# Attention scores as three fp32r products of split operands, in a two-layer gMLP and attention trunk

## The reference

```python
z = h @ w_in[l]                                  # columns: u | v | q | k | value
q = apply_rope(q, cos, sin) * (DIFF_QK_DIM ** -0.5)
k = apply_rope(k, cos, sin)
# 4 heads, each with two halves j of 64 channels; 4 blocks i of 128 query rows
s = jnp.einsum('bqhjd,bkhjd->jbhqk', qb, k)
s = jnp.where(mask, s, NEG_INF)                  # causal by chunks of 64
p = jax.nn.softmax(s, axis=-1)
a = p[0] - lam * p[1]
o = jnp.einsum('bhqk,bkhe->bqhe', a, v)
```

## Time and profile before

| | us |
|---|---|
| median of 3 runs | 1102.96 (1102.85 to 1103.02) |
| the profiled execution | 1103.02 |
| its span, first to last instruction | 1101.1 |
| PE busy | 1088.6 |
| DVE, ACT, POOL busy | 588.4, 577.4, 573.5 |

### The profile page before, as it was taken

How to read it: one execution, slowest core, us unless ns; L and a number is a source line. 1 busy time by engine, 2 the same in 40 slices (tenths; PEclk the granted TensorE clock), 3 DMA queues, 4 the chain that set the end, 5 groups by cost and what they waited for, 6 DMA issues and landing times.

```text
span 1101.1 us, 17399 instructions
## 1 busy us (share of the span) xinstructions
PE 1088.6 (99%) x6765; PEld 962.0 (87%) x6765; DVE 588.4 (53%) x989; ACT 577.4 (52%) x1129; POOL 573.5 (52%) x451
## 2 busy tenths in 40 slices
PE   8999999999999999999999999999999999999998
PEld 6877778999999999888887787789999999998886
DVE  4353535788888885000254445548888888830103
ACT  5656584565555554222356557746555555531212
POOL 4534354666666665544434324645666666646440
PEclk9999999999999999999999999999999999999999
DMA  8323113414333333622243221133333433363212
GB/s 277 123 70 96 58 58 96 154 54 120 96 116 113 92 103 139 218 99 97 77 128 125 77 76 61 60 97 128 105 101 102 116 105 92 112 207 118 96 57 77
DMA packets 144778, 118.33 MB, mean 107 GB/s; under 512 B 3748, under 2 KB 119990, under 8 KB 144695
## 3 DMA queue, kind: packets, MB, share of 16 engines
q1 hardware_dynamic: 144692, 117.20, 34.0%
q10 hardware_dynamic: 2, 0.00, 0.0%
HBM read 110.90 MB, written 6.29 MB: 106 GB/s over the span
## 4 chain that ended last, share of the span: by engine, by line
PE 97%; ACT 1%; issue 0%; DVE 0%; DMA 0%; POOL 0%; DVEq 0%; ACTq 0%
PE banks L583 30%; PE banks L585 30%; PE banks L584 30%; PE banks L642 2%; PE banks L672 2%; PE banks L592 1%; PE banks L657 1%; PE banks L686 1%; PE banks L827 0%; PE banks L693 0%; ACT swap L1155 0%; DMA v_att<-in_pre_mix_g_dram 0%; ACT w_hi L1090 0%; POOL w_lo L514 0%; PE banks L902 0%
## 5 line engine op out<-in xcount | busy, mean ns | idle before, releaser
L514 POOL TENSOR_TENSOR w_lo<-raw,w_hi 128x512 fp32r<-128x512 f32 x204 | 259.5, 1295 | 303.9 <-ACT w_hi L1028 303.9
L532 POOL TENSOR_TENSOR w_lo<-raw,w_hi 128x512 fp32r<-128x512 f32 x200 | 259.9, 1309 | 145.2 <-ACT w_hi L1090 140.6
L583 PE MATMUL banks<-xg_hi,w_hi 128*128 128x256 f32 (+1 forms) x896 | 278.1, 310 | 2.3 <-ACT m L1323 2.3
L585 PE MATMUL banks<-xg_lo,w_hi 128*128 128x256 f32 (+1 forms) x896 | 274.4, 306 | 0.0
L584 PE MATMUL banks<-xg_hi,w_lo 128*128 128x256 f32 (+1 forms) x896 | 274.0, 306 | 0.0
L1028 ACT ACTIVATE w_hi<-raw 128x1024 fp32r<-128x1024 f32 x102 | 106.9, 1056 | 170.7 <-PE banks L585 154.4
L1090 ACT ACTIVATE w_hi<-raw 128x512 fp32r<-128x512 f32 x200 | 125.3, 630 | 121.9 <-DVE raw L1678 64.9
L583 PEld LDWEIGHTS banks<-xg_hi,w_hi 128*128 128x128 f32 x896 | 171.2, 191 | 13.0 <-issue 3.3
L585 PEld LDWEIGHTS banks<-xg_lo,w_hi 128*128 128x128 f32 x896 | 171.2, 191 | 8.1
L584 PEld LDWEIGHTS banks<-xg_hi,w_lo 128*128 128x128 f32 x896 | 171.3, 191 | 6.5
L583 PE MATMUL banks<-w_hi,hid_hi 128*128 128x512 f32 x352 | 137.2, 390 | 0.0
(11 more groups left out here) (164 smaller groups left out, 1848.1 us busy)
## 6 DMA issues: line engine op xcount, KB each, us to landing
raw<-in_w_gate_up_dram SPq DMA_DIRECT2D x88, 512.0 KB, 4.0
raw<-in_w_down_dram SPq DMA_DIRECT2D x44, 512.0 KB, 3.5
raw<-in_w_in_dram SPq DMA_DIRECT2D x40, 512.0 KB, 3.7
raw<-in_w_out_dram SPq DMA_DIRECT2D x16, 512.0 KB, 3.5
x_spill<-x_rows SPq DMA_DIRECT2D x8, 512.0 KB, 4.9
x_rows<-x_spill SPq DMA_DIRECT2D x8, 512.0 KB, 5.5
x_rows<-in_x_dram SPq DMA_DIRECT2D x4, 512.0 KB, 7.5
out_dram<-x_rows SPq DMA_DIRECT2D x8, 256.0 KB, 2.1
```

Of the source, the lines that this page charges most:

```text
L514: last = tt(lo[:, piece], raw_half(l, c, h)[:, piece], hi[:, piece].bitcast(F32), ALU.subtract)
L532: tt(lo, full, hi.bitcast(F32), ALU.subtract).then_inc(w_ready, 1)
L583: mm(o, stat[0], mov[0], start=first, stop=False)
L585: return mm(o, stat[0], mov[1], start=False, stop=last)
```

## The change

The three changes belong together:

- The scores become split products. `rotate` now leaves its sum in the PSUM bank. A new ACT copy, `rotated_high(n)`, rounds it into `k_rot` or `q_rot` (now fp32r), and a new DVE subtraction, `rotated_low(n)`, writes the low part into `k_low` or `q_low`, which are other names for `ya_hi` and `ya_lo`. `gated_high(g)` therefore waits for the last scores of head g.
- A score step issues six matmuls, three passes over the two halves j, the halves alternating, at a width of at least 256 columns (block 0 was 128 wide). All that waited for `qk_rotated` on PE waits for `qk_ready`, which `rotated_low` raises.
- On PE, `scores` 0 and 1 stand half a tile (12 products) later, and `scores` 2 with `turn` 0 as well; `scores` 3 and all that follows stay. On DVE `maxima(0)` stands behind the two first `normalize_gate`.

```diff
-                for j in range(2):
-                    ps = slice(j * HD, (j + 1) * HD)
-                    last = mm(bank[SC_BANKS[n % 2][j]][:, 0:w], q_rot[ps, h, i * P:(i + 1) * P], k_rot[ps, h, 0:w],
-                              start=True, stop=True)
+
+                w = max(w, 2 * P)
+                for n_pass, (q, k) in enumerate(((q_rot, k_rot), (q_low, k_rot), (q_rot, k_low))):
+                    for j in range(2):
+                        ps = slice(j * HD, (j + 1) * HD)
+                        last = mm(bank[SC_BANKS[n % 2][j]][:, 0:w], q[ps, h, i * P:(i + 1) * P], k[ps, h, 0:w],
+                                  start=(n_pass == 0), stop=(n_pass == 2))
...
                 qk_half(l, 2, lower)
                 qk_half(l, 2, upper)
+                qk_half(l, 3, lower)
                 scores(l, 0)
-                qk_half(l, 3, lower)
+                qk_half(l, 3, upper)
                 scores(l, 1)
-                qk_half(l, 3, upper)
+                va(C_VA, 0, (0, 1))
                 scores(l, 2)
                 turn(l, 0)
-                va(C_VA, 0, (0, 1))
                 va(C_VA, 1, (0, 1))
                 scores(l, 3)
...
+                def rotated_high(n):
+                    act.wait_ge(qk_rotated, 8 * l + n + 1)
+                    col, h = QK_TILES[n]
+                    fn((k_rot if col == K0 else q_rot)[:, h, :], bank[QK_BANKS[n]][:, :], ACT.Copy)\
+                        .then_inc(qk_hi_ready, 1)
...
                 swapped(3)
                 copy_turned(1)
                 exponentials(3)
+                rotated_high(3)
                 copy_values(0)
...
-                    tt(dst, o[:, :], swap[:, n % 2, :], ALU.add).then_inc(qk_rotated, 1)
+                    tt(o[:, :], o[:, :], swap[:, n % 2, :], ALU.add).then_inc(qk_rotated, 1)
+
+                def rotated_low(n):
+                    dve.wait_ge(qk_hi_ready, 8 * l + n + 1)
+                    col, h = QK_TILES[n]
+                    hi, lo = (k_rot, k_low) if col == K0 else (q_rot, q_low)
+                    tt(lo[:, h, :], bank[QK_BANKS[n]][:, :], hi[:, h, :].bitcast(F32), ALU.subtract)\
+                        .then_inc(qk_ready, 1)
...
                 rotate(3)
                 maxima(3)
                 combine(3)
+                rotated_low(3)
                 maxima(4)
...
                 rotate(5)
                 add_terms(1)
+                rotated_low(5)
                 maxima(8)
                 add_terms(2)
                 rotate(6)
                 maxima(9)
+                rotated_low(6)
                 add_terms(3)
```

More of the change, by code:

```diff
@@ L137, in trunk @@
         rs_x = sb("rs_x", [P, ST])
+        k_low, q_low = ya_hi, ya_lo
         xn = scratch
@@ L232, in trunk @@
         qk_rotated = sem("qk_rotated")
+        qk_hi_ready = sem("qk_hi_ready")
+        qk_ready = sem("qk_ready")
         ws_turned = sem("ws_turned")
@@ L633, in scores @@
                 if i == 0:
-                    pe.wait_ge(qk_rotated, 8 * l + 2 * h + 2)
+                    pe.wait_ge(qk_ready, 8 * l + 2 * h + 2)
                 if n == 0:
@@ L648, in turn @@
                 if n == 0:
-                    pe.wait_ge(qk_rotated, 8 * l + 3)
+                    pe.wait_ge(qk_ready, 8 * l + 3)
                 elif n == 6:
@@ L712, in u_half @@
                     if t < 2:
-                        pe.wait_ge(qk_rotated, 8 * l + 7 + t)
+                        pe.wait_ge(qk_ready, 8 * l + 7 + t)
                     else:
@@ L890, in _ @@
                 scores(l, 4)
-                pe.wait_ge(qk_rotated, 8 * l + 4)
+                pe.wait_ge(qk_ready, 8 * l + 4)
                 pe.wait_ge(tables_landed, 16 * 3 * (l + 1))
@@ L1224, in _ @@
                 swapped(1)
+                rotated_high(0)
                 high(l, 4, 1)
+                rotated_high(1)
                 swapped(2)
@@ L1228, in _ @@
                 high(l, 5, 0)
+                rotated_high(2)
                 exponentials(1)
@@ L1258, in _ @@
                 copy_turned(6)
+                rotated_high(4)
                 take_heads(2)
@@ L1262, in _ @@
                 swapped(5)
+                rotated_high(5)
                 take_heads(3)
@@ L1266, in _ @@
                 high(l, 9, 0)
+                rotated_high(6)
                 exponentials(9)
@@ L1269, in _ @@
                 high(l, 9, 1)
+                rotated_high(7)
                 copy_turned(8)
@@ L1476, in rotate @@
                     col, h = QK_TILES[n]
-                    dst = (k_rot if col == K0 else q_rot)[:, h, :]
                     o = bank[QK_BANKS[n]]
@@ L1559, in _ @@
                 rotate(1)
+                rotated_low(0)
+                rotated_low(1)
                 if l == 0:
@@ L1569, in _ @@
                     dve.wait_ge(par_ready, 1 + 2 * L)
-                maxima(0)
                 dve.wait_ge(ln_root_ready, l + 1)
@@ L1575, in _ @@
                 normalize_gate(1)
+                maxima(0)
                 rotate(2)
                 combine(0)
+                rotated_low(2)
                 maxima(1)
@@ L1599, in _ @@
                 combine(7)
+                rotated_low(4)
                 rotate(5)
                 add_terms(1)
+                rotated_low(5)
                 maxima(8)
@@ L1610, in _ @@
                 maxima(10)
+                rotated_low(7)
                 combine(10)
```

7 lines of the change are left out of this document (4 added, 3 removed).

## The result

The changed kernel takes 1109.99 us (median of 5 runs, 1107.12 to 1111.43) beside 1102.96 for the kernel before (1102.81 to 1103.16) on the same chip: ratio 1.0064, 95% interval 1.0052 to 1.0075. It is slower, as forecast, by 7.0 us where 5.6 were forecast; the median lies just inside the forecast's own range of 1107 to 1110. The profiled execution took 1109.99 us.

The account below looks back on a forecast made before the run. PE's issue and waits were taken as the bound: waits +7.5, scores -1.7, lost wait -0.2, together +5.6 us on 1103.02, giving 1108.6 us; own range 1107 to 1110 (72%), 8 in 10 from 1105.5 to 1114.5.

Parts of the forecast that it names:

- fifth step: Fifth score step in each layer: PE waits 2.37 us for tile 3's low part behind combine(3), its chain starting at turn(0).
- ninth step and `u_half(0)`: PE waits for low parts in each layer: 0.81 us at head 2's first score step, 0.57 us at u_half(0).
- score steps: All score steps, three fp32r passes instead of two fp32: 0.57, 0.57, 0.735, 0.90 us by width; -1.7 us for eight heads.
- first step's wait of before: PE's 0.22 us wait ahead of layer 0's first score step goes, as that step stands 12 products later; -0.2 us.
- PE's issue and PE's waits make up the time: Whole kernel: PE busy 1088.6 of 1101.1 us; new ACT and DVE work costs only where PE waits for its chain.
- The rival with hidden slack: Chain behind turn(0) has unseen slack, so the fifth score step does not wait: 1103.9 us, within 0.2%; chance 8%.
- The two smaller waits: PE's waits for low parts at the ninth score step, 0.81 us, and at u_half(0), 0.57 us, in each layer.
- The rival by which the change is faster: Draining around score steps belongs to fp32 and goes, saving up to 0.34 us a step: 1097.7 us; chance 4%.
- Loads hidden in fp32r too: In score steps the two halves still stream side by side in fp32r, only the first weight load visible; 0.21 us fixed.
- the first in the list of rivals: Weight loads show in every score pass: steps of 0.73, 0.73, 0.89, 1.05 us, 1113.3 us in all; chance 9%.
- The rival in which the halves do not overlap: Score steps' two halves run in series in fp32r: 0.93, 0.93, 1.26, 1.59 us a step, 1121.7 us; chance 7%.
- a lower clock as a sign of being wrong: A lower granted clock behind a PE wait of 2.4 us would show the forecast wrong; no size given.

Follow-up runs that it names:

- experiment 1: Changed kernel with tile 3's ACT copy ahead of exponentials(3) and its DVE low part ahead of combine(3); 1102.58 us, ratio 1.0008 to the kernel before.
- experiment 6: Changed kernel with PE's order of the kernel before, maxima(0) left in its new place; 1106.44 us, ratio 1.0037 to the kernel before.
- experiment 3: Kernel before with only the new order on PE and maxima(0) moved on DVE, scores whole in fp32; 1101.53 us, ratio 0.9995.
- Experiments 5: Changed kernel with tile 3's two moves, and on ACT swapped(5) ahead of high(8, 1) and copy_turned(7), swapped(6) ahead of take_heads(3); 1103.17 us, ratio 1.0006.
- Experiment 9: Changed kernel with tile 3's two moves, swapped(6) ahead of take_heads(3) on ACT, gate of block 2 ahead of scores(l, 8) on PE; 1100.47 us, ratio 0.9985.
- experiment 4: Changed kernel with each score step's three passes of half 0 issued before the three of half 1; 1111.14 us, ratio 1.0080 to the kernel before.
- experiment 8: The changed kernel itself, unaltered, timed again on another set of runs; 1109.70 us, ratio 1.0064 to the kernel before.

## Why the prediction was right, and where its sum was short

The forecast and what the two traces and the runs show, for both layers:

| term | forecast, us | shown, us |
|---|---|---|
| fifth step | +4.7 | +4.5 (2.27 a layer, experiment 1) |
| ninth step and `u_half(0)` | +2.8 | idle 2 x (0.76 + 0.26), with restarts +2.8 (experiment 1) |
| score steps | -1.7 | -2.0, with what the products around them lose about -1.8 |
| first step's wait of before | -0.2 | -0.2 |
| clock behind the fifth step | none | +1.6 each time it falls |
| start of the kernel | none | +0.2 in this pair |

- **PE's issue and PE's waits make up the time**: right. The busy times of DVE and ACT rose by 9.0 and 7.9 us and cost nothing as such; experiment 1 keeps all of that work and is within 0.1% of before.
- **The fifth step**: right in place, cause and size. The chain behind `turn(0)` has no slack: 2.23 us idle against a forecast lateness of 2.37. That the order on PE makes it is shown by experiment 6 (without the move the fifth step does not wait), that it takes the low part too by experiment 3. The rival with hidden slack falls.
- **What the move buys**: a gap in the working. I priced the move's cost at the fifth step and never what it avoids at the first. Experiment 6 shows 1.59 and 0.53 us there. This left the sum right, since the change contains the move, but it would have misjudged a variant.
- **The two smaller waits**: right. PE is idle 0.76 and 0.26 us there. The idle time is counted from the end of the last record (0.39 us long), before which the next product would have started without a wait (0.23 us behind the last start), so the price is higher. It shows in experiment 1, layer 0: from the first of the 12 products ahead of the ninth step to the step 3.74 us (109.96 to 113.70) against 2.91 in the kernel before (111.45 to 114.36), so 0.83 where 0.81 was forecast; from the first of the 12 products ahead of `u_half(0)` to behind its own 12, 6.14 us (121.11 to 127.25) against 5.58 (121.72 to 127.30), so 0.56 where 0.57 was forecast. Experiments 5 and 9 take both away.
- **The score steps**: right to 0.1 us, slightly mis-sized. I added 0.21 to three product distances and had 0.57, 0.735, 0.90; shown are 0.55, 0.72, 0.89. All 32 steps, from start to next start, take 23.68 us in the trace before and 21.71 after. With the clock and the waits set apart, experiment 1's marks give 1.8 us net for the two layers: 245.15 - 15.97 - 228.94 = +0.24 and 786.85 - 245.15 - 541.21 = +0.49, of which about 1.4 a layer are the two smaller waits as measured above and, in layer 0, -0.22 the lost one; what is left is -0.9 in each. The rival by which the change is faster falls too: the fixed part of a step is still 0.2 us (0.89 less three product distances), and the 12 products behind a step take 2.99 us (58.07 to 61.06) where they took 2.95.
- **Loads hidden in fp32r too.** The row that answers to the earlier trace rows, weight loads of the 512-wide step after the change:

```profile
68.34 0.19 PEld L649 LDWEIGHTS banks<-k_rot,q_rot 64*128 64x128 f32 x2 [0.35 <-issue]
68.44 0.19 PEld L649 LDWEIGHTS banks<-k_rot,ya_lo 64*128 64x128 f32 x2
68.68 0.19 PEld L649 LDWEIGHTS banks<-ya_hi,q_rot 64*128 64x128 f32 x2
```

The second pair of loads begins 0.1 us after the first pair, while the first pass holds the same rows until 68.67, and the third pass follows the second at 0.24 us, the plain product distance: no load shows. The rule of the Trainium skill ("TensorE: Matmul & The Clock Gate", packing small matmuls) by which a weight load overlaps matmuls in flight only when its row group is another one would have shown one in each pass; this trace does not agree, and that rival falls (it is the first in the list of rivals; where the prediction speaks of the skill it calls it the second). The rival in which the halves do not overlap falls with the same rows, and experiment 4 adds that the overlap does not need alternating halves.

- **The clock**: the term that was missing. I had named a lower clock as a sign of being wrong and gave it no price. It comes in some executions and not in others: one fall in the first profiled run of this kernel, two in the second, with the waits 2.2 us in all four places. Each costs about 1.6 us: layer 1 takes 545.63 us with a fall (experiment 8) and 543.97 without. The first five runs line up with it: mean clock of the whole run 0.999 and 1107.12 us, 0.998 and 1109.99, 0.997 and 1110.01 or 1109.67, 0.996 and 1111.43. This is a hint only, since the mean clocks of single runs of the kernel before lie between 0.998 and 1.000 as well, with no fall in the attention parts of its one profiled run. Without a fall the table gives 1103.02 + 4.5 + 2.8 - 1.8 - 0.2 = 1108.3 for the profiled pair, 0.3 under the forecast. The Trainium skill says on the same page, in the section on the clock gate, that the clock falls after idleness and that the number of slow products at the start of one and the same kernel differs from run to run. The traces agree with the first, though the page speaks of longer gaps than the 1.59 and 2.23 us behind which the clock fell here. They show the like of the second in mid-kernel: the same waits in layers 0 and 1 are followed by one fall in one run and by two in another.

What stays open: what decides behind which wait the clock falls, since its length alone does not. It fell behind five of the six waits of 2.2 us in the profiled runs of the change and of experiments 4 and 8, behind both of 3.4 and the one of 1.59, and behind none shorter; but also not behind those near the start, 1.6 us in every run (for the DVE tile eps, at 1.6 us) and 1.8 us in experiments 1 and 3. And why the first marks scatter by 1.9 us between profiled runs (15.39 to 17.25, in kernels that don't differ up to there). That is why I compare from mark to mark; I take it for a part of the spread of single runs of every kernel, which is not shown, since each kernel has but one profiled run here (the change two).

## What to carry to other kernels

When a chain of copies ends in a new last link, ask at which place of each engine's list the link stands: here two exchanges of neighbours, an instruction for which PE waits next ahead of one for which it waits later, gave back some 6 us of the 7 (experiment 1, 1.0008 against 1.0064). Price a move at both ends, at the place that comes earlier and at every fixed place whose chain starts in what was moved. And price an idle TensorE above its own length: a wait of 2 us among dense products can cost 1.6 us more behind it (the changed kernel and experiment 8), in busy time, where no list of waits shows it.

## What the runs showed of the hardware that I had not expected

- The granted clock fell from 1.00 to 0.50 (2.4 to 1.2 GHz) behind single waits of PE of 1.6 and 2.2 us in a kernel whose TensorE is busy for 98% of the span. With nine products issued into the wait it did not fall in the profiled run.
- Two matmuls on the upper and the lower half of the rows, in different banks, start together although two others stand between them in the issue order (experiment 4, starts at 68.60 and 68.61; the step takes 0.90 us against 0.89).
- Experiment 9 gains 0.85 and 0.58 us in its layers, where experiment 1 without its waits (1.38 a layer) would gain 1.14 and 0.89. The 0.3 us a layer that are missing stand around the ninth step. The 12 products ahead of the moved gate of block 2 take 3.04 us (110.78 to 113.82) against the 2.91 that they take ahead of the step in the kernel before, with a wait of 0.06 at their end: the gate comes a step earlier now and finds its `v_gate` from DVE (L1558) just late. The gate itself takes 1.09 us (114.91 - 113.82 above) against 0.99, and the weighing behind the step 1.58 (115.46 to 117.04) against 1.48. The kernel before:

```profile
114.78 1.16 PE L686 MATMUL banks<-wsT,v_gate 128*128 128x128 f32 x8
115.77 1.39 PE L672 MATMUL banks<-v_att,attnT 128*128 128x128 f32 x11
```

  So the order of small matmuls has a price of its own, about 0.1 us at each of these two places. I can name the places, not the cause.
